# Summing the modulation's partial products over partitions: the products as moving operand, 64 stationary columns, one turn of rows into columns at the end

## What is computed

```python
silu_c = jax.nn.silu(c)
silu_cc = jax.nn.silu(c_ctx)
for layer in range(DEPTH):
    mod_x = silu_c @ ada_w[layer] + ada_b[layer]
    mod_c = silu_cc @ ada_w[layer] + ada_b[layer]
    sh1, sc1, g1, sh2, sc2, g2 = [m[:, None, :] for m in jnp.split(mod_x, 6, axis=-1)]
    csh1, csc1, cg1, csh2, csc2, cg2 = jnp.split(mod_c, 6, axis=-1)
    hx = modulate(rmsnorm(x, norm1_g[layer]), sh1, sc1)
...
```

## Time and profile before

| | us |
|---|---|
| median of 3 runs | 3759.76 (3759.74 to 3764.34) |
| the profiled execution, its own time | 3764.54 |
| its span in the trace | 3762.7 |
| PE busy | 3543.3 (94%) |
| DVE busy | 2017.1 (54%) |
| ACT busy | 1232.1 (33%) |
| mean granted TensorE clock, share of full | 0.951 |

### The profile page before, as it was taken

How to read it: one execution, slowest core, us unless ns; L and a number is a source line. 1 busy time by engine, 2 the same in 40 slices (tenths; PEclk the granted TensorE clock), 3 DMA queues, 4 the chain that set the end, 5 groups by cost and what they waited for, 6 DMA issues and landing times.

```text
span 3762.7 us, 42305 instructions
## 1 busy us (share of the span) xinstructions
PE 3543.3 (94%) x17448; PEld 2805.7 (75%) x17448; DVE 2017.1 (54%) x3717; ACT 1232.1 (33%) x2053; POOL 212.6 (6%) x302
## 2 busy tenths in 40 slices
PE   7999899999989999998999989999998998879998
PEld 6657678887867678887986557888887885558886
DVE  5565588856654588854126664323235236654344
ACT  4353343234453333233112222332233212134332
POOL 0200000001040000000000001000001000000000
PEclk9999999999999999999999859999999998789999
DMA  4302155522202145533210011212122220112331
GB/s 164 115 12 79 45 168 179 167 91 84 74 27 78 45 157 172 168 119 124 81 57 27 26 38 46 79 57 68 57 66 86 99 68 17 40 45 90 101 91 67
DMA packets 214108, 317.01 MB, mean 84 GB/s; under 512 B 5304, under 2 KB 162618, under 8 KB 212636
## 3 DMA queue, kind: packets, MB, share of 16 engines
q1 hardware_dynamic: 198108, 243.00, 19.9%
q0 software_dynamic: 15808, 71.31, 5.6%
HBM read 300.66 MB, written 14.49 MB: 84 GB/s over the span
## 4 chain that ended last, share of the span: by engine, by line
PE 83%; DVE 11%; ACT 4%; issue 2%; DMA 1%; POOL 0%; SPq 0%; DVEq 0%; ACTq 0%; POOLq 0%
PE ps L94 82%; DVE t L115 5%; ACT t L100 3%; DVE t L107 3%; PE ps L97 1%; DVE t L111 1%; DVE ps L107 0%; DVE ps L115 0%; DVE t L121 0%; DVE t L112 0%; DMA t<-gates_away 0%; DVE t L125 0%; DVE ps L112 0%; DVE t L118 0%; DMA t<-in_mem 0%
## 5 line engine op out<-in xcount | busy, mean ns | idle before, releaser
L94 PE MATMUL ps<-t,t 128*128 128x512 f32 (+7 forms) x17032 | 3486.5, 368 | 193.5 <-DVE t L107 98.1
L94 PEld LDWEIGHTS ps<-t,t 128*128 128x128 f32 (+3 forms) x17032 | 2753.2, 191 | 900.4 <-issue 177.3
L100 ACT ACTIVATE t<-t 128x1024 fp32r<-128x1024 f32 (+6 forms) x1168 | 831.0, 744 | 1226.7 <-PE ps L94 653.5
L107 DVE TENSOR_TENSOR t<-t,t 128x1024 fp32r<-128x1024 f32 (+5 forms) x882 | 781.7, 911 | 708.9 <-ACT t L100 693.5
L100 ACT ACTIVATE t<-ps 128x512 f32<-128x512 f32 (+5 forms) x490 | 248.5, 531 | 1062.7 <-PE ps L94 1027.7
L115 DVE SCALAR_TENSOR_TENSOR t<-t,t,t 128x256 f32<-128x256 f32 (+4 forms) x935 | 438.7, 530 | 7.6 <-ACT t L100 1.2
L107 DVE TENSOR_TENSOR t<-ps,t 128x512 f32<-128x512 f32 (+4 forms) x293 | 187.4, 659 | 248.2 <-PE ps L94 181.8
L115 DVE SCALAR_TENSOR_TENSOR t<-ps,t,t 128x512 f32<-128x512 f32 (+1 forms) x228 | 139.7, 662 | 279.7 <-PE ps L94 259.6
L107 POOL TENSOR_TENSOR t<-t,t 128x64 f32<-128x64 f32 (+1 forms) x196 | 129.3, 684 | 1724.9 <-ACT t L100 1721.6
L118 DVE COPY t<-ps 128x256 f32<-128x256 f32 (+3 forms) x169 | 75.9, 477 | 276.8 <-PE ps L94 256.7
L100 ACT ACTIVATE t<-ps,t 128x512 f32<-128x512 f32 (+3 forms) x106 | 61.6, 582 | 131.9 <-PE ps L94 94.6
(11 more groups left out here) (31 smaller groups left out, 293.3 us busy)
## 6 DMA issues: line engine op xcount, KB each, us to landing
t<-in_w_ff SPq DMA_DIRECT2D x64, 1024.0 KB, 7.6
t<-in_w_mlp SPq DMA_DIRECT2D x64, 1024.0 KB, 5.4
t<-in_ada_w POOLq DMA_DIRECT2D x48, 1024.0 KB, 5.9
t<-in_w_in SPq DMA_DIRECT2D x30, 1024.0 KB, 5.3
t<-in_w_qkv_o SPq DMA_DIRECT2D x12, 1024.0 KB, 5.1
t<-in_w_mem_kv SPq DMA_DIRECT2D x8, 1024.0 KB, 6.0
t<-in_w_mem_q SPq DMA_DIRECT2D x8, 1024.0 KB, 5.1
t<-in_w_mem_o SPq DMA_DIRECT2D x8, 1024.0 KB, 5.1
```

What stands on the lines that cost most here:

```text
L94: return Issued(self, self.e and self.e.matmul(o, l, r, start=start, stop=stop, skip_group_check=True))
L100: return Issued(self, self.e and self.e.activation(o, i, f, **kw))
L107: return Issued(self, self.e and self.e.tensor_tensor(o, a, b, op))
```

## The change

The sum over partitions turns round. At step s TensorE now issues one fp32 matmul: `ACC` (128 x 512: both vectors, 256 columns each) is the moving operand, and the stationary one is a slice of 64 columns of a new constant `band` (128 x 127, ones in column 63, else zero). The slice `[64 - s : 128 - s]` has its ones in column s - 1, so step s adds the sums of block s - 1 to row s - 1 of bank 2 and zeros to the other rows. All 24 steps accumulate into bank 2, rows 0 to 63. At step 24 DVE copies rows 0 to 23 to a new tile `ROWS`, TensorE turns them into columns of bank 7 by four fp32 matmuls against a 24x24 identity, and DVE adds the bias with two instructions of 128x48. DVE's two additions per step go, and its wait for TensorE's sum of the block just before; before it overwrites an `ACC` it waits for the sum that read it.

```diff
@@ constants
-        ("LE", 128), ("GE", 128), ("GT", 128), ("LT", 128), ("sel", 208)]
+        ("LE", 128), ("GE", 128), ("GT", 128), ("LT", 128), ("sel", 208), ("band", 127)]
@@ feed_forward, TensorE
+                if s == 1:
+                    opening(2)
                 pe.wait_ge("macc", l, s - 1, 1)
-                opening(7)
-                for m in range(2):
+                pe.matmul(P[2][0:64, :], cst("band")[:, 64 - s:128 - s], tiles.ACC[(s - 1) % 2][:, :, :], s == 1, s == 24).then_inc(
+                    "mps", l, s - 1)
+                if s == 24:
+                    opening(7)
+                    pe.wait_ge("mod_rows", l)
                     for c in range(2):
-                        ins = pe.matmul(P[7][:, 2 * m + c:2 * m + c + 1], tiles.ACC[(s - 1) % 2][:, c, 128 * m:128 * m + 128],
-                                        cst("ones", 128, 1), True, True)
-                ins.then_inc("mps", l, s - 1)
-                free[7] = [("mod", l, s - 1)]
+                        for m in range(2):
+                            ins = pe.matmul(P[7][:, 48 * c + 24 * m:48 * c + 24 * m + 24],
+                                            tiles.ROWS[:, 256 * c + 128 * m:256 * c + 128 * m + 128], cst("ident", 24, 24), True, True)
+                    ins.then_inc("mod_cols", l)
+                    free[2], free[7] = [("mod_rows", l)], [("mod", l)]
@@ feed_forward, VectorE
-                if s > 0:
-                    dve.wait_ge("mps", l, s - 1)
-                    for m in range(2):
-                        k = 2 * (s - 1) + m
-                        ins = dve.tensor_scalar(MOD[l][:, k, :], P[7][:, 2 * m:2 * m + 2], vec(f"ada_b{l}", k), None, ALU.add)
-                        if m == 0:
+                if s == 24:
+                    dve.wait_ge("mps", l, 23)
+                    dve.tensor_copy(tiles.ROWS[:, :], P[2][0:24, :]).then_inc("mod_rows", l)
+                    dve.wait_ge("mod_cols", l)
+                    for c in range(2):
+                        ins = dve.tensor_tensor(MOD[l][:, :, c].rearrange("p (s m) -> p s m", m=2),
+                                                P[7][:, 48 * c:48 * c + 48].rearrange("p (m s) -> p s m", m=2),
+                                                vec(f"ada_b{l}", 0, 48).rearrange("p (s m) -> p s m", m=2), ALU.add)
...
                 if s < 24:
+                    if s > 1:
+                        dve.wait_ge("mps", l, s - 2)
```

More of the change, by code:

```diff
@@ L439, in ff_area @@
             f.ADA = [ar([128, 2048]) for _ in range(2)]
-            f.ACC = [ar([128, 2, 256]) for _ in range(2)]
+            f.ACC, f.ROWS = [ar([128, 2, 256]) for _ in range(2)], ar([24, 512])
         return f
@@ L1850, in modulate @@
                     return
-                if s > 0:
-                    dve.wait_ge("mps", l, s - 1)
-                    for m in range(2):
-                        k = 2 * (s - 1) + m
-                        ins = dve.tensor_scalar(MOD[l][:, k, :], P[7][:, 2 * m:2 * m + 2], vec(f"ada_b{l}", k), None, ALU.add)
-                        if m == 0:
+                if s == 24:
[6 more added lines that the diff above has]
+                                                vec(f"ada_b{l}", 0, 48).rearrange("p (s m) -> p s m", m=2), ALU.add)
+                        if c == 0:
                             ins.then_inc()
                         else:
-                            ins.then_inc("mod", l, s - 1)
+                            ins.then_inc("mod", l)
                 if s < 24:
+                    if s > 1:
+                        dve.wait_ge("mps", l, s - 2)
                     wv = tiles.ADA[s % 2][:, :].rearrange("p (k n) -> p k n", k=8)
@@ L2138, in modulation @@
         def modulation(which, name):
-            dve.wait_ge("mod", l, 23)
+            dve.wait_ge("mod", l)
             o = 24 * which
@@ L2671, in constants @@
     c["sel"] = sel.reshape(128, 208)
+    c["band"] = np.broadcast_to(np.arange(127)[None, :] == 63, (128, 127))
     out = {"cst": np.concatenate([np.asarray(c[n], f4) for n, _ in CSTS], 1)}
```

## The result

Four executions of the changed kernel took 3775.06, 3787.82, 3789.92 and 3790.65 us, a median of 3788.87; four of the kernel before beside them took 3759.74 to 3764.34. The ratio is 1.0057, with an interval of 1.0041 to 1.0074: slower, by 0.4 to 0.7%. The profiled execution is the one of 3775.06 us, with a span of 3773.3 and a mean clock of 0.952. That one lies on the forecast of 3774.8; the other three, and the median, lie above its range of 3764 to 3784.

What follows compares the result with a forecast made beforehand. TensorE was taken to bound the feed-forward stages. A layer: steps 6.6, waits -2.3, step 24 +3.1, together 7.4 us; two layers 14.8 and constants 0.2 make +15.0, so 3774.8 us, range 3764 to 3784.

Steps and rivals of the forecast that it cites:

- The price of the step: TensorE's matmul between two units: new step 1.20 us for the old 0.90, 0.34 of it for the change of shape.
- the prediction's estimate: One-column matmuls at about 60 cycles: old step's eight records 0.2 us, kernel dearer by some 45 us; not used.
- The waits: TensorE's waits for DVE: five of 0.40 us at steps 4 to 20 go, with step 1's 0.30: 2.3 us a layer.
- Step 24: Once a layer TensorE idles some 2.1 us for DVE's additions and copy, then turns the rows: 3.1 us more in all.
- my second rival: The clock falls in step 24's wait, costing 2.3 to 3.8 us a layer, about 3781 us; chance 0.14.
- The rest of the kernel within 1 us: Outside the two feed-forward stages, the kernel's time was to stay within 1 us of the kernel before.
- the larger constant: Constants that land ahead of the first transpose grow by 64 KB: 0.2 us more.
- Slower by over 0.2%: Sign for the whole kernel: slower 0.81, same 0.16, faster 0.03; under 0.2% (7.5 us) counts as the same.
- The first rival: The switch of shape costs nothing at the steps, each 0.04 us cheaper; kernel at 3761.4 us, time unchanged; chance 0.13.
- the third: Passes get cheaper alone, 0.22 us each: step 0.78 us, 0.12 cheaper than before, no change in time; chance 0.04.

Runs made afterwards that it cites:

- e2: Changed kernel with 128 stationary columns in place of 64 (band of 255 columns); median 3776.10 us, ratio 1.0003 to 1.0042 to the kernel before.
- e5: Kernel before, each step writing its own four columns of bank 7, bias added once at step 24; median 3766.80 us, ratio 0.9968 to 1.0012.
- e3: Changed kernel with TensorE's turning matmuls and the bias additions one unit later, at step 25; median 3784.55 us, ratio 1.0032 to 1.0067 to the kernel before.
- d1: Changed kernel with one matmul ahead of the late stage issued three more times, 0.70 us; median 3781.70 us, ratio 1.0037 to 1.0062 to the kernel before.
- a1: The changed kernel measured again, with no further edit; median 3788.58 us, ratio 1.0027 to 1.0076 to the kernel before.
- b1: Kernel before with only the new constant added, never read; median 3763.65 us, ratio 0.9989 to 1.0016.
- b2: Kernel before with two more one-column matmuls at every step, 0.45 us a step; median 3775.85 us, ratio 1.0007 to 1.0041.
- d2: Kernel before with one matmul ahead of the late stage issued 12 more times, 2.80 us; median 3775.94 us, ratio 1.0031 to 1.0058.
- e4: Changed kernel with e2's and e3's edits together, the turn on all 128 rows; median 3773.35 us, ratio 1.0006 to 1.0045 to the kernel before.

## Why the prediction was right, and where it was not

**The price of the step: right.** Periods of 12.39 us were forecast and measured; e2 took the change of shape away alone and 0.33 us went with it. The exchange of a 128-column for a 64-column stationary operand costs 0.34 us in and out here, read beforehand from rows of another stage. The Trainium skill's TensorEngine Tiling (Array Packing), section Key Properties, says that a change of mode drains TensorE; the trace of the changed kernel agrees, with 0.09 us more than the usual 0.233 ahead of the first 64-column pass. By the prediction's estimate from the same page's section Instruction Overhead the new step would have been 1.0 us dearer than the old; the runs say 0.30.

**The waits: right.** All of those at steps 4 to 20 are gone in the changed kernel; in e2, where the step is short again, 0.20 us a time are back, and e5 shows that they answer to DVE's 0.26 us.

**Step 24: the wait right, its price too small.** 1.80 us of idle time for 2.1 forecast, but the clock fell behind it in both layers. That was my second rival, with a chance of 0.14, held for the lesser case because full matmuls preceded the wait. The copy took 0.67 us on 24 partitions, for 0.69 taken from copies on 128. The low clock costs 1.5 us a layer, for 2.3 to 3.8 expected. With it a stage should be 7.4 + 1.5 = 8.9 us longer; measured are 8.8 to 9.4 in two profiles. e3 shows that without the wait the fall doesn't come; that the wait doesn't bring it every time is shown by d1, whose first layer has the same 1.8 us of idle time, no fall, and a stage 1.4 us shorter.

**"The rest of the kernel within 1 us": wrong.** This is the term that failed. I carried the sum over as if what no edit touches kept its time. The rest took 8.0 us less in the first profile and 7.1 more in a1's (span less both stages: 3042.3 before, 3034.3, 3049.4). In a1's profile the late stage is 12.1 us longer than the kernel before's and all else outside the stages 5.0 shorter. So the first profile met the forecast of 3774.8 by luck, with 18.6 - 8.0, two deviations that cancel in part, and the median of 3788.87, 14 us above it, is the usual case of the changed kernel: all six executions of a1 were above 3782. The two stages alone, 17.6 to 18.6 us over the kernel before's median of 3760.3, would give 3777.9 to 3778.9. The ratio's middle, 1.0057, stands for 3781.7 us, inside the range of 3764 to 3784; its ends are 3775.7 and 3788.1. The 3 us between these two come from the rest of the kernel, and so does the end beyond the range. The 0.2 us for the larger constant are not to be seen in b1.

**The sign and the rivals.** Slower by over 0.2% was given 0.81 and came. The first rival (no price for the switch) and the third (cheap lone passes) are refuted by the periods.

**What stays open.** Why the first fall of the clock comes where it does in one execution and not in the next, and why the changed kernel and e5, with the same first fall at 54.8, have late stages of 436.9 and 450.6 us (the low clock that begins there lasts 13.7 us in the one and 44.4 in the other). How much of the 12 to 15 us belongs to this change in the long run, and how much would fall to any edit that moves the arrival by a part of a microsecond, the runs don't say: b2 is as long in the stages and was spared. No version that was tried is measurably faster than the kernel before.

## What to carry to other kernels

Before a small matmul is put between large ones, compare the shape of its stationary operand with theirs: 64 columns between 128 cost 0.34 us a time here, more than was saved by going from eight weight loads to two, and 128 columns, all but one of them zeros, were 0.33 us cheaper than 64. A turn or a copy that another engine must do first belongs one unit behind its cause, so that the bounding engine doesn't stand idle, above all since 1.8 us of idle time was, seven times in eight, counting e2's 2.3, followed by 3.4 us of half clock. And where a kernel has a stage in which TensorE's clock goes up and down, compare stages and not totals: a total moved by 12 us through 2.8 us of work elsewhere (d2).

## What the runs showed of the hardware that was not expected

- A stretch of some 200 us, in which TensorE often waits, took 197.7 to 212.5 us for the same work in thirteen profiles, in groups that agree within 0.2 us (197.8, 205.0, 209.4, 212.4, and 211.3 once). In the eleven with a fall of the clock near 11 us, a few tenths of a microsecond in its place went with up to 14.7 us of length. 0.70 us more work ahead of it (d1) went with 11.6 us less than in a1, though the changed kernel's first profile was as short without it; 2.80 us more (d2) with 11.5 us more than in the kernel before.
- An idle time of 1.80 us (2.26 in e2) between stretches of full 512-column matmuls was followed by a clock of 0.50 for 3.4 us in both layers of the changed kernel's two profiles and of e2's, and in one of the two layers of d1's; without the wait (e3, e4) never.
- A pass of 512 fp32 columns takes 0.43 us with 64 stationary columns in a pair (208.40 to 208.83 in the earlier trace rows) and with 128; alone with 64 columns it is spaced 0.48 and 0.52 (593.29, 593.77, 594.29), which is 0.43 and the exposed loads and drain.
